# Query, key and value projections of a sparse-attention block computed token by token in 512-column products

## The reference

```python
h = rmsnorm(x, norm1_w)
P = h @ w_in                              # one combined projection
q = rmsnorm(q_in.reshape(b, s, 8, 128), q_norm_w)
kc_raw, vc_raw, ks, vs, kw, vw = jnp.split(kv_in, 6, axis=-1)   # 2 groups x 128 each
kc = rmsnorm(compress(kc_raw, ...), k_norm_w[0])   # compressed keys
ks = rmsnorm(ks, k_norm_w[1])             # keys of the selected branch
kw = rmsnorm(kw, k_norm_w[2])             # keys of the local (window) branch
o  = g0 * att(q, kc, vc) + g1 * att(q, ks, vs) + g2 * att(q, kw, vw)
```

## Time and profile before

| | |
|---|---|
| median of 3 runs | 570.16 us (570.06 to 571.1) |
| the profiled execution's own time | 570.36 us |
| its span, first to last instruction | 568.4 us |
| PE busy | 561.1 us (99%) |
| DVE busy | 388.7 us (68%) |
| ACT busy | 305.4 us (54%) |
| POOL busy | 71.5 us (13%) |

### The profile page before, as it was taken

How to read it: one execution, slowest core, us unless ns; L and a number is a source line. 1 busy time by engine, 2 the same in 40 slices (tenths; PEclk the granted TensorE clock), 3 DMA queues, 4 the chain that set the end, 5 groups by cost and what they waited for, 6 DMA issues and landing times.

```text
span 568.4 us, 9793 instructions
## 1 busy us (share of the span) xinstructions
PE 561.1 (99%) x3894; PEld 494.7 (87%) x3894; DVE 388.7 (68%) x619; ACT 305.4 (54%) x491; POOL 71.5 (13%) x85
## 2 busy tenths in 40 slices
PE   8999999999999999999999999999999999999997
PEld 7999999899898898788888888898888888888885
DVE  4879987849665744899784665667675656657564
ACT  3768568714345646664745443465545454454541
POOL 3111220972800000017000000000000000000000
PEclk9999999999999999999999999999999999999999
DMA  7944488195894441442444464664667675657722
GB/s 242 306 151 149 149 201 248 57 290 171 211 273 156 149 153 70 149 149 78 146 151 146 148 220 154 197 171 149 177 193 206 169 216 172 198 167 204 194 103 74
DMA packets 99398, 98.17 MB, mean 173 GB/s; under 512 B 4834, under 2 KB 83863, under 8 KB 99354
## 3 DMA queue, kind: packets, MB, share of 16 engines
q1 hardware_dynamic: 97040, 93.63, 53.8%
q0 software_dynamic: 1808, 2.78, 2.5%
q10 hardware_dynamic: 506, 1.14, 0.6%
HBM read 96.39 MB, written 1.84 MB: 173 GB/s over the span
## 4 chain that ended last, share of the span: by engine, by line
PE 94%; DVE 2%; DMA 1%; ACT 1%; issue 0%; ACTq 0%; DVEq 0%
PE ps L1474 19%; PE ps L1476 18%; PE ps L1475 18%; PE ps L1582 14%; PE ps L1585 7%; PE ps L1479 4%; PE ps L1705 4%; PE ps L1854 2%; PE ps L1828 2%; PE ps L1557 1%; DMA rows_b<-in_cmp_pe 1%; PE ps L1730 1%; PE ps L1739 1%; PE ps L1851 1%; PE ps L1673 1%
## 5 line engine op out<-in xcount | busy, mean ns | idle before, releaser
L988 DVE TENSOR_TENSOR w_lo<-raw,w_hi 128x2048 fp32r<-128x2048 f32 x75 | 173.7, 2317 | 96.5 <-ACT w_hi L633 96.4
L633 ACT ACTIVATE w_hi<-raw 128x2048 fp32r<-128x2048 f32 x75 | 143.4, 1912 | 77.9 <-PE ps L1476 67.9
L1582 PE MATMUL ps<-h_both,w_hi 128*128 128x512 f32 x352 | 122.5, 397 | 0.5 <-issue 0.5
L1585 PE MATMUL ps<-h_both,w_lo 128*128 128x256 f32 x352 | 91.2, 279 | 0.3 <-DVE h_both L1014 0.3
L1474 PE MATMUL ps<-h_both,w_hi 128*128 128x256 f32 x272 | 77.9, 286 | 0.2 <-issue 0.2
L1475 PE MATMUL ps<-h_both,w_hi 128*128 128x256 f32 x272 | 76.9, 283 | 0.0
L1476 PE MATMUL ps<-h_both,w_lo 128*128 128x256 f32 x272 | 76.9, 283 | 0.0
L1582 PEld LDWEIGHTS ps<-h_both,w_hi 128*128 128x128 f32 x352 | 63.8, 188 | 14.1 <-issue 2.0
L1585 PEld LDWEIGHTS ps<-h_both,w_lo 128*128 128x128 f32 x352 | 66.4, 188 | 4.0 <-issue 0.6
L1474 PE MATMUL ps<-w_hi,h_both 128*128 128x512 f32 (+1 forms) x160 | 58.2, 364 | 0.3 <-DVE zs L1328 0.2
L1476 PE MATMUL ps<-w_hi,h_both 128*128 128x512 f32 (+1 forms) x160 | 55.6, 348 | 0.0
(11 more groups left out here) (382 smaller groups left out, 962.1 us busy)
## 6 DMA issues: line engine op xcount, KB each, us to landing
raw<-in_w_in SPq DMA_DIRECT2D x31, 1024.0 KB, 5.3
raw<-in_w_gate SPq DMA_DIRECT2D x22, 512.0 KB, 4.0
raw<-in_w_up SPq DMA_DIRECT2D x22, 512.0 KB, 5.3
raw<-in_w_down SPq DMA_DIRECT2D x11, 1024.0 KB, 4.9
raw<-in_cmp_w SPq DMA_DIRECT2D x8, 1024.0 KB, 8.2
raw<-in_w_proj_a SPq DMA_DIRECT2D x4, 1024.0 KB, 5.4
raw<-in_w_proj_b SPq DMA_DIRECT2D x4, 1024.0 KB, 5.1
raw<-in_w_out SPq DMA_DIRECT2D x4, 1024.0 KB, 5.1
```

The lines of the kernel that those rows point to most:

```text
L633: nc.scalar.activation(w_hi[s % NSPL][:], raw[RAW_OF[n]][:], ACT.Copy).then_inc(hi_done, 1)
L988: nc.vector.tensor_tensor(w_lo[s % NSPL][:], raw[RAW_OF[n]][:], w_hi[s % NSPL][:].bitcast(f32), ALU.subtract).then_inc(lo_done, 1)
L1582: cross = lambda stop: pe.matmul(banks[part][:], hi[:, k, part * P:(part + 1) * P], h_both[:, :, k, :], start=(k == 0), stop=stop)
L1585: end = pe.matmul(banks[part][:, 0:SEQ], lo[:, k, part * P:(part + 1) * P], h_hi[:, k, :], start=False, stop=False)
```

## The change

- nq, ks/vs and kw/vw become wide kinds. nq 0/1 and nq 2/3 are two pairs; ks and vs become the pair sv 0, sv 1 (keys and values side by side as 512 columns, in two halves of the rows), kw and vw the pair wv 0, wv 1. They take the slots of the old chunks: sv 0 for ks, sv 1 for kw, wv 0 for vs, wv 1 for vw.
- Queries come out token by token. For each half ACT makes four squares of 128 columns with a sum (`accum_out`) into `rn` and one copy to nq_tok; PE turns nq_tok with 8 transposes for each pair (`turn_q`) and ACT copies the turned queries to nqT (`turned_q`, two copies for each pair). The sums over partitions, their turning, their copy and a small POOL memset go.
- For each half of sv and wv ACT makes two copies of 256 columns, key_tok and values. After the second half it squares the keys into sc[0] or sc[1], for which it now waits until W2_K is out.
- keys(0) moves from the start of slot ks+1 to the start of slot cmpv 0, keys(1) to slot gz 0, TURN_KW from slot vw to slot gz 1, behind TURN_PC in the count.

```diff
-TOKEN_MAJOR = ("ks", "vs", "kw", "vw", "wo")
+TOKEN_MAJOR = ("wo",)
-WIDE_KINDS = ("gz", "mga", "pa", "mgb", "pb")
+WIDE_KINDS = ("sv", "wv", "nq", "gz", "mga", "pa", "mgb", "pb")
...
-EARLY_SPLIT = {AT["cmpk", 0]: AT["nq", 0], AT["nq", 1]: AT["nq", 2], AT["nq", 3]: AT["ks", 0], AT["kw", 0]: AT["vs", 0],
-               AT["vs", 0]: AT["vw", 0], AT["vw", 0]: AT["gz", 0], AT["gz", 0]: AT["gz", 1]}
+EARLY_SPLIT = {AT["cmpk", 0]: AT["nq", 0], AT["nq", 1]: AT["nq", 2], AT["nq", 3]: AT["sv", 0], AT["sv", 1]: AT["wv", 0],
+               AT["wv", 0]: AT["wv", 1], AT["wv", 1]: AT["gz", 0], AT["gz", 0]: AT["gz", 1]}
...
-W2_K, TURN_KC, TURN_KS, LOGITS_C, TURN_KW, TURN_LC, TURN_PC, W2_V = range(8)
+W2_K, TURN_KC, TURN_KS, LOGITS_C, TURN_LC, TURN_PC, TURN_KW, W2_V = range(8)
+MISC_SLOTS = {W2_K: (AT["sv", 1], 0), TURN_KC: (AT["wv", 0], 0), TURN_KS: (AT["wv", 0], 1), LOGITS_C: (AT["cmpv", 1], 1),
+              TURN_KW: (AT["gz", 1], 0), TURN_LC: (AT["wv", 1], 1), TURN_PC: (AT["gz", 0], 1), W2_V: (AT["gz", 3], 0)}
...
+TURN_Q = {(AT["nq", 2], 1): 0, (AT["sv", 0], 0): 1}
+Q_OUT = {(AT["nq", 3], 0): 0, (AT["sv", 0], 1): 1}
...
+                if kind == "nq":
...
+                    for q in range(4):
+                        h = 2 * (i - 1) + q
+                        nc.scalar.activation(sc[0][:, q // 2, q % 2 * P:(q % 2 + 1) * P], bank[:, q * P:(q + 1) * P], ACT.Square,
+                                             accum_out=col["rn"][:, h, t:t + 1]).then_inc(nq_sq, 1)
+                    nc.scalar.activation(nq_tok[i // 2][:, t, :], bank[:], ACT.Copy).then_inc(copied, 1)
+                if kind in ("sv", "wv"):
+                    act.wait_ge(half_done, 2 * n + 1 + t)
+                    bank = stream_ps[(BANK_USE[n] + t) % 2]
+                    a, values = (0, vs) if kind == "sv" else (1, vw)
+                    nc.scalar.activation(key_tok[:, a, 2 * t:2 * t + 2, :].rearrange("p g d -> p (g d)"), bank[:, 0:CW], ACT.Copy).then_inc(key_copied, 1)
+                    nc.scalar.activation(values[:, t, :, :].rearrange("p g d -> p (g d)"), bank[:, CW:], ACT.Copy).then_inc(copied, 1)
+                    if t == 1:
+                        act.wait_ge(key_copied, 2 * a + 2)
+                        act.wait_ge(m_out, W2_K + 1)
+                        nc.scalar.activation(sc[a][:].rearrange("p a c -> p (a c)"), key_tok[:, a, :, :].rearrange("p a d -> p (a d)"),
+                                             ACT.Square).then_inc(key_in, 1)
...
+            def turned_q(p):
+
+                for c in range(2):
+                    act.wait_ge(nq_turned, 2 * p + c + 1)
+                    nc.scalar.activation(nqT[:, 4 * p + 2 * c:4 * p + 2 * c + 2, :].rearrange("p h c -> p (h c)"), gdn_ps[c][:],
+                                         ACT.Copy).then_inc(nq_out, 1)
...
-                    if n == AT["ks", 0] + 1:
+                    if n == AT["sv", 1] + 1:
                         keys(0)
...
-                        if n == AT["vs", 0]:
+                        if n == AT["wv", 1] + 2:
                             keys(1)
...
+            def turn_q(p):
+                pe.wait_ge(copied, COPY_NO[AT["nq", 2 * p + 1]] + 1)
...
+                for c in range(2):
+                    if p == 1:
+                        pe.wait_ge(nq_out, c + 1)
+                    for q in range(4):
+                        h, t = 2 * c + q // 2, q % 2
+                        last = transpose(gdn_ps[c][:, q * P:(q + 1) * P], nq_tok[p][:, t, h * P:(h + 1) * P])
+                    last.then_inc(nq_turned, 1)
...
-                    if n in (6, 10, AT["ks", 0]):
-                        head_sums({6: 0, 10: 1}.get(n, 2), half)
+                    if n in (6, 10):
+                        head_sums({6: 0, 10: 1}[n], half)
+                    if (n, half) in TURN_Q:
+                        turn_q(TURN_Q[n, half])
```

More of the change, by code:

```diff
@@ L55, in weight_chunks @@
     out += [("kc", 0), ("vc", 0), ("cmpk", 0), ("cmpk", 1), ("nq", 0), ("nq", 1), ("cmpk", 2), ("nq", 2), ("nq", 3), ("cmpk", 3)]
-    out += [("ks", 0), ("kw", 0), ("cmpv", 0), ("vs", 0), ("cmpv", 1), ("vw", 0), ("cmpv", 2), ("gz", 0), ("cmpv", 3)]
+    out += [("sv", 0), ("sv", 1), ("cmpv", 0), ("wv", 0), ("cmpv", 1), ("wv", 1), ("cmpv", 2), ("gz", 0), ("cmpv", 3)]
     out += [("gz", i) for i in range(1, 4)]
@@ L254, in hybrid_block @@
         csum = ar(6, "csum", (P, 2 * SEQ), off=4 * KB)
-        nsq = [ar(5, f"nsq{i}", (P, 2, SEQ), off=i * 2 * KB) for i in range(4)]
+        nq_tok = [ar(5, f"nq_tok{i}", (P, TT, 2 * CW), off=i * 4 * KB) for i in range(2)]
         ya_hi, ya_lo = ar(5, "ya_hi", (P, KT, SEQ), f32r), ar(6, "ya_lo", (P, KT, SEQ), f32r)
@@ L408, in wait_bank @@
             if kind in COPIED:
-                eng.wait_ge(copied, COPY_NO[m] + 1)
+                eng.wait_ge(copied, COPY_NO[m] + part + 1)
             elif kind in ("mga", "mgb"):
@@ L720, in evacuate @@
                     ins.then_inc(copied, 1)
[L721 to L733, removed]
                 elif kind in ("kc", "vc"):
@@ L936, in _ @@
                         split_mix(MIX_TURNS[n])
+                    if (n, half) in Q_OUT:
+                        turned_q(Q_OUT[n, half])
                     if half == 1 and n in LATE_IN_SLOT:
@@ L1661, in head_sums @@
                 if half == 0:
[L1662 to L1667, removed]
+                    pe.wait_ge(conv_sq, 4 * (j + 1))
                     pe.wait_ge(ones_set, 2)
@@ L1670, in head_sums @@
                         pe.wait_ge(csum_out, j)
-                    squares, one = (nsq, ones_nq[:]) if j == 2 else (csq, ones_sq[:, 0:32])
                     for i in range(4):
-                        last = pe.matmul(ps[5][32 * i:32 * i + 32, :], one, squares[i][:].rearrange("p a c -> p (a c)"), start=True, stop=True)
+                        last = pe.matmul(ps[5][32 * i:32 * i + 32, :], ones_sq[:, 0:32], csq[i][:].rearrange("p a c -> p (a c)"), start=True, stop=True)
                     last.then_inc(csum_mm, 1)
@@ L1679, in head_sums @@
                     for i in range(4):
-                        last = transpose((ps[7] if j == 2 else ps[6])[:, i * P:(i + 1) * P], (csum_n if j == 2 else csum)[:, i * P:(i + 1) * P])
+                        last = transpose(ps[6][:, i * P:(i + 1) * P], csum[:, i * P:(i + 1) * P])
                     last.then_inc(csum_tr, 1)
@@ L1725, in gdn @@
                             pe.wait_ge(diag_in, 32 * NSUB)
+                            pe.wait_ge(nq_out, 4)
                         else:
@@ L1768, in gdn @@
                     last.then_inc(g_mm, 1)
+            def turn_q(p):
+                pe.wait_ge(copied, COPY_NO[AT["nq", 2 * p + 1]] + 1)
+                if p == 0:
+                    for b in range(1, NB):
+                        wait_use(pe, "kq", b)
+                for c in range(2):
[5 more added lines that the diff above has]
+                    last.then_inc(nq_turned, 1)
             def turn_o(b):
@@ L1808, in misc @@
                 elif m == LOGITS_C:
-                    pe.wait_ge(copied, COPY_NO[AT["nq", 3]] + 1)
+                    pe.wait_ge(nq_out, 4)
                     for c in range(4):
@@ L1825, in unit @@
                     else:
-                        pe.wait_ge(m_out, TURN_PC + 1)
+                        pe.wait_ge(m_out, TURN_KW + 1)
                     for a, keys in enumerate((ksT, kwT)):
```

38 lines of the change are left out of this document (17 added, 21 removed).

## The result

The kernel became slower: 576.41 us median (574.91 to 576.57) against 570.56 us before in the same comparison, ratio 1.0093 [1.0075, 1.011]. The profiled execution took 576.41 us, its span is 574.4 us against 568.4. The forecast was 573.2.

The account below looks back on a forecast made before the run. PE's own sequence, 94% of the chain, was taken as the bound. X4's new wait starts wv 0 3.4 us later, its halves return 0.4: +3.0, so 573.4 profiled, 573.2 median; range 571.6 to 574.6, eight in ten 571.0 to 576.5.

Parts of the forecast that it names:

- a standstill of 4.3 us: In X4, PE would stand still from the third block's end, about 161.4, until ACT's copy at 165.7.
- the gap slows PE afterwards: Rival: behind the wait in X4 PE returns at the lower clock level, at most 3.2 us more, 576.4; chance 0.18.
- The argument from the opening: The granted clock does not mark the slow opening (40 matmuls in 7.66 us), which speaks against reading it as lower level.
- 0.18 against 0.63: Chance that the gap also slows PE, against chance of the forecast, a wait at X4 within 571.6 to 574.6.
- L: Landing time of wv 0's weight load, which sets the wait at X4: taken as 156.9, bounds 155.3 to 158.3.
- the forecast's sum: Landing 156.9 through m_out at 164.54 to wv 0's half 0 at 166.24: +3.0 us in all, 573.4 profiled.
- the lower bound: Earliest landing of wv 0's load, 155.3, at the clean stretch's rate behind cmpv 0; gives 571.6 us.
- the place of the wait: One new PE wait inside X4, at its fourth block, ended by ACT's copy held behind m_out.
- 7.64: From wv 0's load landing to m_out on DVE: 0.06 us to the high part, then 7.58.
- the 3 to 5.5 named: Sign of being right: PE has one wait of 3 to 5.5 us inside X4, no other over 0.5.
- second wait: Claimed absent: keys(0) ends about 168.6, before half 0 of wv 0 at 169.2, so Y4's writing is not held.
- PE's own saving ahead of X4: Wide halves and dropped head sums less the queries' transposes: 0.9 us less PE time before X4.

Follow-up runs that it names:

- e7: The changed kernel, wait kept, with 15 unused matmuls in PE's gap ahead of X4's fourth block: 572.31 us, ratio 1.0026.
- e8: The changed kernel with wv 0 loaded in two transfers with rows of 1 KB: 575.55 us, ratio 1.0085.
- e2: The kernel before with one line added, ACT waiting for m_out before it squares kw's keys: 577.16 us, ratio 1.0113.
- e5: The changed kernel with an own scratch tile for W2_K, no m_out wait, and keys(0) behind Y4's writes on DVE: 569.39 us, ratio 0.9976.
- e6: The changed kernel, wait and shared scratch kept, with W2_K ahead of wv 0's low part on DVE: 569.41 us, ratio 0.9975.
- e9: e6 with 26 opening matmuls in place of 20 (52 records for 40): 568.63 us, ratio 0.9967.
- e3: The changed kernel, wait kept, with 30 unused matmuls ahead of X4's fourth block, longer than the gap: 575.71 us, ratio 1.0082.
- e4: The changed kernel with the unused POOL memset of the opening put back: 575.43 us, ratio 1.0077.
- e10: The changed kernel with 26 opening matmuls in place of 20 (52 records for 40): 575.04 us, ratio 1.0075.
- e1: The changed kernel with a scratch tile of its own for W2_K and no ACT wait for m_out: 570.52 us, ratio 0.9986.

## Why the prediction was wrong

**The step that failed** is the choice between two prices for the gap. The prediction saw a standstill of 4.3 us, named "the gap slows PE afterwards" with a price of at most 3.2 us and a chance of 0.18, and kept the forecast at the upper level because the granted clock "does not mark that opening". The runs show the rival: 0.50 granted from 166.2 to about 171.5 behind the gap, 2.6 us in the profile of the change, 3.0 in e8, and 572.31 instead of 575.55 us when the gap is filled (e7 against e8). So the price was near (at most 3.2), the weight given to it was not.

The argument from the opening misread its row. The granted clock does stand at 1.00 all through the opening of before, but the matmuls don't run at one pace there (stretches of before, one and the same string):

```profile
6.00:7.00 1.00, 1.00 (x7) 1.00 (x7) 0.89 (x5) 0.72 (x2) 0.00 (x0) 1.00 0.82 219
7.00:8.00 1.00, 1.00 (x10) 1.00 (x10) 0.83 (x6) 0.00 (x0) 0.00 (x0) 1.00 0.89 292
```

In the trace some 28 of the 40 records start 0.21 us apart and the rest 0.11, close to the 0.43 against 0.23 behind the gap in X4. So the row doesn't mark a stretch that has the pace of the lower level, and what was read as speaking against the rival spoke, if anything, for it: PE began at that pace, out of standing still. Whether a gap of 4 us in the middle of the kernel leads back to it, the trace of before couldn't tell, as it has no such gap; so it was no reason for 0.18 against 0.63.

The Trainium skill, "TensorE: Matmul & The Clock Gate", section "HAM oscillation — how this bites in real kernels", describes this pattern: short bursts of matmuls with waits between them, after which the array is back at the lower rate. By that rule the rival holds, and the trace of the change agrees: 0.43 us between matmuls behind the gap against 0.23 without it.

With that term and L's 0.44 the forecast's sum is 573.4 + 2.6 + 0.4 = 576.4 for the profiled execution, which took 576.41. With the early opening it is 573.4 - 1.6 (L = 155.3) + 3.0 = 574.8, and the profiled execution of e8 took 574.95.

**L.** 157.34 is near the 156.9 taken, by luck. The load took 10.5 us from its issue where I reckoned 11.5 from 145.4, and the late opening pushed the issue to 146.85. With an early opening L is 155.3 (e7, e8), the lower bound. Why the load is quicker than vs's 12.9 stays open. The Trainium skill, "DMA: Bandwidth & Descriptors", section "Queues, rings and completion order", says that a DMA engine alternates between queues packet by packet; that longer rows would win more of it was a step the prediction added. e8 shows no such effect (10.6 us with short rows, 10.5 with long). The kernel before with one wait added (e2) has 11.4 where before has 12.9, so it also varies with no change in the loads.

**Right:** the place of the wait, its releaser, and each link: 7.61 us from landing to m_out (7.64 in the forecast's sum; the 7.58 named beside it counts from the start of the high part), and PE's wait of 3.6 us inside the 3 to 5.5 named. No second wait arose: from Y4 to the end it is 0.37 us less, where 0.3 was forecast. keys(1) and TURN_KW moved at no cost: the only waits left are those of the earlier trace rows. The queries' turns took 0.88 us for eight, as reckoned; their squares with a sum came 0.25 us apart where 0.38 was taken from the earlier trace rows, and held nobody.

**Mis-sized, but hidden:** PE's own saving ahead of X4. From the turns of xn to X4 it is 160.82 - 11.44 = 149.38 us before and 158.84 - 11.02 = 147.82 in e7, 1.56 us less where 0.9 was forecast. Most of the rest is the halves: 2.94 us for one in e7, not 2.97, makes some 0.4 us over the twelve ahead of X4. The wait swallowed the saving. It is what e5, e6 and e9 win.

**Not the change's:** the late opening in the profile of the change. PE is quicker through the 40 records (6.26 us), pauses 2.54 us, and falls to the lower level about 1.3 us after it is back; X4 starts at 160.65 to 160.98 us in the profiles of the changed kernel and its variants with a late opening and at 158.82 to 159.21 in those with an early one (e3, e5, e7, e8), 1.4 to 2.2 us apart. L moves with it, so the wait is the same (3.6 us in the change, 3.7 in e8).

## What to carry to other kernels

When a wait is added ahead of an engine's in-order queue, look at everything that is queued behind it, and at what the awaited result is itself queued behind: here a scratch tile shared by two small jobs tied TensorE to a weight load, and moving one job ahead of a split freed it without another buffer. A standstill of TensorE can have two prices, the wait and the lower level afterwards; where the trace has no gap of that length, whether the second is due is unknown, and it belongs in the sum with weight of its own. Read the pace of TensorE from the starts of like matmuls and not from the granted clock alone. Before reading a difference of two profiles, compare their openings and ends, since a microsecond or two may be neither's doing.

## What the runs showed of the hardware

- A wait of 3.3 to 3.9 us in X4 was followed by the lower level in every profile that had one (the change, e2, e4, e8, e10); the wait of 1.16 us in Y4 of e1 was not. It lasted until about 170.7 us in e10 and 171.5 in the change, and half 0 behind it took 4.9 to 5.4 us for 2.97 (in e2, with 256 columns, 4.6 for 3.05).
- In e2 the granted clock fell only after PE had run again for about 1.2 us; in the change it had fallen before PE was back (0.79 in the mean of the gap).
- The 40 records of the opening took 6.1 to 7.7 us from execution to execution, as the pace rose from 0.21 to 0.11 us earlier or later (behind some 14 of them in the change, 28 before). In the main, the quicker they were, the longer PE stood still for the load behind them: 7.66 and a pause of 0.95 us before, 6.26 and 2.54 in the change. Pauses of 2.3 to 2.6 us (the change, e1, e2, e4, e6) were followed by slow turns, those up to 1.5 us were not. The stretch behind it ran at 0.66 to 0.72 in the change and at 1.00 in e10, where no pause is left:

```profile
10.00:12.50 2.50, 2.26 (x10) 1.44 (x10) 1.24 (x3) 0.55 (x1) 0.00 (x0) 0.72 0.66 172
12.50:15.50 3.00, 3.00 (x20) 3.00 (x20) 0.93 (x3) 1.80 (x5) 0.00 (x0) 0.66 1.09 362
```
```profile
10.00:12.50 2.50, 2.50 (x18) 1.75 (x18) 1.24 (x3) 0.41 (x2) 0.00 (x0) 1.00 0.63 166
12.50:15.50 3.00, 3.00 (x28) 3.00 (x27) 2.26 (x5) 3.00 (x7) 0.07 (x1) 1.00 1.09 363
```

These are the stretches from 10 to 15.5 us of the change, then of e10, with the columns of the earlier trace rows.
